# Leaving out the filler products on TensorE between the sums of the block boundaries

## The reference: what is computed

```python
def rmsnorm(x, g):
    xf = x.astype(jnp.float32)
    y = xf * lax.rsqrt(jnp.mean(xf * xf, axis=-1, keepdims=True) + EPS)
    return (y * g.astype(jnp.float32)).astype(x.dtype)

def swiglu(h, w_in, w_out):
    gate, up = jnp.split(h @ w_in, 2, axis=-1)
    return (jax.nn.silu(gate) * up) @ w_out

def sandwich(x, y_fn, g_pre, g_post, shift, scale, gate, resid_w):
    h = rmsnorm(x, g_pre) * (1.0 + scale) + shift
    return x + resid_w * gate * rmsnorm(y_fn(h), g_post)
```

## Time and profile before

| what | value |
| --- | --- |
| time, median of 3 runs | 3115.12 us (3114.57 to 3115.67) |
| span of the profiled execution | 3107.6 us |
| PE busy, share of the span | 2975.6 us, 96% |
| DVE busy | 1610.7 us, 52% |
| ACT busy | 1023.3 us, 33% |
| TensorE's mean granted clock | 0.988 of full |
| DMA, mean | 105 GB/s |

### The profile page before, as it was taken

One profiled execution on the slowest core, in us unless ns is written; L12 is line 12 of the kernel. 1 busy time (PEld: TensorE's weight loads), 2 busy tenths in 40 slices (PEclk: granted clock), 3 DMA queues, 4 the chain that ended last, 5 costly groups with the idle time before them and its releaser, 6 DMA issues.

```text
span 3107.6 us, 39441 instructions
## 1 busy us (share of the span) xinstructions
PE 2975.6 (96%) x13288; PEld 2336.5 (75%) x13288; DVE 1610.7 (52%) x2438; ACT 1023.3 (33%) x1693; POOL 167.5 (5%) x131
## 2 busy tenths in 40 slices
PE   5999999999999999999979999999999999999997
PEld 3888867677768777888858888677777778688885
DVE  5655436667444636633255553466665365465323
ACT  2322224444334323222232222344433343232321
POOL 0111010000000001110011100100000000111100
PEclk9999999999999999999989999999999999999999
DMA  5644422111212223533225543221111123154232
GB/s 200 217 175 169 142 70 82 48 48 52 65 48 88 94 77 132 185 102 102 88 84 195 189 166 112 70 68 55 48 55 62 63 78 104 48 195 164 94 96 74
DMA packets 88008, 326.76 MB, mean 105 GB/s; under 512 B 10016, under 2 KB 10400, under 8 KB 86944
## 3 DMA queue, kind: packets, MB, share of 16 engines
q1 hardware_dynamic: 87840, 324.63, 30.6%
HBM read 322.49 MB, written 2.10 MB: 104 GB/s over the span
## 4 chain that ended last, share of the span: by engine, by line
issue 65%; PE 32%; POOL 1%; DVE 1%; ACT 0%; DVEq 0%; POOLq 0%; ACTq 0%
PE bank L426 10%; PE bank L427 10%; PE bank L428 10%; POOL x L530 1%; PE bank L1580 1%; POOL rstd_tok L523 1%; PE bank L1542 0%; DVEq L1178 0%; DVE diag L1114 0%; DVE h_low L1125 0%; DVE norm_tmp L1130 0%; ACT h_high L770 0%; DVE x L1179 0%; DVE ffn_act L1281 0%; ACT ffn_high L816 0%
## 5 line engine op out<-in xcount | busy, mean ns | idle before, releaser
L426 PE MATMUL bank<-h_high,w_high 128*128 128x512 f32 x2384 | 955.7, 401 | 8.8 <-DVE h_low L1125 8.8
L428 PE MATMUL bank<-h_high,w_low 128*128 128x512 f32 x2384 | 934.9, 392 | 0.0
L427 PE MATMUL bank<-h_low,w_high 128*128 128x512 f32 x2384 | 934.3, 392 | 0.0
L410 DVE TENSOR_TENSOR w_low<-w_raw,w_high 128x1024 fp32r<-128x1024 f32 x440 | 567.9, 1291 | 698.2 <-ACT w_high L404 697.2
L404 ACT ACTIVATE w_high<-w_raw 128x1024 fp32r<-128x1024 f32 x440 | 462.3, 1051 | 402.3 <-PE bank L428 402.3
L426 PEld LDWEIGHTS bank<-h_high,w_high 128*128 128x128 f32 x2384 | 452.2, 190 | 113.6 <-DVE h_low L1125 16.2
L428 PEld LDWEIGHTS bank<-h_high,w_low 128*128 128x128 f32 x2384 | 450.9, 189 | 97.2
L427 PEld LDWEIGHTS bank<-h_low,w_high 128*128 128x128 f32 x2384 | 452.3, 190 | 91.8 <-issue 2.2
L426 PE MATMUL bank<-ffn_high,w_high 128*128 128x512 f32 x704 | 280.6, 399 | 0.0
L428 PE MATMUL bank<-ffn_high,w_low 128*128 128x512 f32 x704 | 274.2, 390 | 0.0
L427 PE MATMUL bank<-ffn_low,w_high 128*128 128x512 f32 x704 | 274.2, 389 | 0.0
(11 more groups left out here) (195 smaller groups left out, 2917.3 us busy)
## 6 DMA issues: line engine op xcount, KB each, us to landing
w_raw<-stream SPq DMA_DIRECT2D x444, 512.0 KB, 3.5
ada_raw<-ada SPq DMA_DIRECT2D x144, 512.0 KB, 3.5
ada_start<-ada SPq DMA_DIRECT2D x4, 2048.0 KB, 16.3
mixer_consts<-mixc SPq DMA_DIRECT2D x2, 1152.0 KB, 5.2
x<-x_in SPq DMA_DIRECT2D x1, 2048.0 KB, 16.3
out<-x SPq DMA_DIRECT2D x8, 256.0 KB, 2.2
lru_w<-lruw SPq DMA_DIRECT2D x2, 512.0 KB, 3.7
all_par<-pars SPq DMA_DIRECT2D x1, 163.0 KB, 2.4
```

Of the source, the lines that this page charges most:

```text
L410: eng.tensor_tensor(wL[:, slot], raw[:, slot], wH[:, slot].bitcast(F32), ALU.subtract).then_inc(lo_ready[slot].sem, 1)
L426: eng.matmul(o, a, rhs_h, start=first, stop=False)
L427: eng.matmul(o, a, rhs_l, start=False, stop=False)
L428: return eng.matmul(o, b, rhs_h, start=False, stop=last)
```

## The change

The calls of `keep_warm`, the function itself, its table of counts and the wait for the ring slot that the fillers read are taken out. Nothing else is edited: the wait on `y_saved` that stood ahead of the fillers stays.

```diff
-WARM = (10, 16, 1, 11, 6)
...
-            def keep_warm(n, times):
-
-
-                slot = (U_MIX if n == 0 else U_FFN[1]) % RING
-                for _ in range(times):
-                    pe.matmul(bank[7][:, :], wH[:, slot, 0:P], wH[:, slot, 0:T], start=True, stop=True)
-
             def end_of_boundary(l, n):
                 for j in range(4, KD):
                     sum_squares(l, sq_at(n, 0) + j, False, j == KD - 1)
                 if n < NB - 1:
                     pe.wait_ge(y_saved.sem, y_saved.at(l, 4 * n + 4))
-                    unit_ready(pe, l, U_MIX if n == 0 else U_FFN[1])
-                    keep_warm(n, WARM[0])
                 pe.wait_ge(diag_ready.sem, diag_ready.at(l, norm_at(n, 0) + 1))
                 spread(l, n, diag[:, :, :].rearrange("p t n -> p (t n)"), 5)
                 if n < NB - 1:
-                    keep_warm(n, WARM[1])
                     pre_norm(l, n)
 
             def pre_norm(l, n):
                 for j in range(KD):
                     sum_squares(l, (sq_at(n, 1) if n >= 0 else -KD) + j, j == 0, j == KD - 1)
-                    if n >= 0 and j % 2 and j < KD - 1:
-                        keep_warm(n, WARM[2])
-                if n >= 0:
-                    keep_warm(n, WARM[3])
                 pe.wait_ge(diag_ready.sem, diag_ready.at(l, (norm_at(n, 1) if n >= 0 else -1) + 1))
                 spread(l, n, diag[:, :, :].rearrange("p t n -> p (t n)"), 6)
-                if n >= 0:
-                    keep_warm(n, WARM[4])
```

## The result

The changed kernel takes 3125.75 us in the median of five runs (3123.97 to 3127.34), the kernel before 3114.66 us (3113.24 to 3115.67) beside it. The ratio is 1.0037 with a 95% interval of 1.0024 to 1.0049: slower by 7.5 to 15.3 us, with 11.1 us between the medians. The forecast was 3125.3 us.

A forecast was written before the change was run, and what follows sets the result against it. PE was taken to bound the blocks, while engines take turns at boundaries. Mixer boundaries at 2.05 us and FFN boundaries at 3.05 us, each twice, add 10.2 us: 3115.1 to 3125.3 us, range 3119.5 to 3131.5 us.

The forecast's parts named there:

- Boundary n = 2 is the model: Boundary n = 2 never had fillers; its two stretches at 0.53 clock were taken to show what the changed boundaries will do.
- sums of x: Matmul group between the two spreads of a boundary: 0.1 us lost, at most 0.6, as the clock returns within it.
- second spread: Matmul group between the last sums of x and the first product: DVE waits 0.45 us longer, between 0 and 0.95.
- first spread: Matmul group ahead of the sums of x in a boundary: DVE waits 0.3 us longer, between 0.09 and 0.94.
- entry to the mixer: First products after boundary n = 0: 1.2 us lost, between 0.65 and 1.7, with 1.0 us hidden behind DVE.
- entry to an FFN: First product to first gate after boundary n = 1, where PE is the bound: 2.2 us lost, between 1.66 and 2.72.
- 0.47 us lost for each us at half clock: Price under dense matmuls, from the FFN entry behind boundary n = 2: 1.66 us lost over some 3.5 us of products.
- The 7.5 us around the span: Time outside the profiled span, said to stay: span 3107.6 to 3117.8 us, median 3115.1 to 3125.3 us.
- The rival on the mixers' own falls: Clock falls inside the mixers land elsewhere: 5.5 us regained, 3119.8 us, chance 0.11; or worse, 3130.8 us, chance 0.11.
- A flat price for half-clock time: Rival: each us at 1.2 GHz costs 0.5 us, idle or not; four boundaries cost 40 us, 3155 us; chance 0.02.
- The clock holds: Rival: sums and spreads alone hold the full clock at n = 0 and 1, so 3115 us; chance 0.02.
- one group alone is cold: Rival: only the entries to the mixer and FFN are slow, 6.8 us in all, 3121.9 us; chance 0.07.

The follow-up runs named there:

- the second trace: The changed kernel run once more with no edit, beside the kernel before: 3126.2 us, ratio 1.0045 (1.0033 to 1.0057).

## Why the prediction was right, point by point

- *Nothing waits for the fillers.* Right: no stretch of a changed boundary got shorter by more than 0.04 us.
- *Boundary n = 2 is the model.* Right: two stretches at half clock in each changed boundary, and full clock in between from the middle of the sums of x. It hasn't "the same steps in the same times", though. In the kernel before, PE idled 5.90 us there ahead of the second spread, in the changed boundaries 2.85 us; the clock fell in both.

```profile
1585.87 2.08 PE L1542 MATMUL bank<-diag,ones 128*128 128x512 f32 x2 [5.90 <-DVE diag L1114]
```
- *The terms.* Over the eight changed boundaries of the two traces of the changed kernel:

| term | forecast | mean measured | smallest, largest |
| --- | --- | --- | --- |
| first spread | 0.3 | 0.27 | 0.0, 0.95 |
| sums of x | 0.1 | -0.03 | -0.04, -0.01 |
| second spread | 0.45 | 0.47 | 0.0, 0.95 |
| entry to the mixer | 1.2 | 1.16 | 0.47, 1.64 |
| entry to an FFN | 2.2 | 2.41 | 1.50, 2.92 |
| four boundaries | 10.2 | 10.0 | 9.6, 10.4 |

  The two bounds for an FFN entry, 1.66 and 2.72 us, were a little narrow: 1.50 and 2.92 us were seen. Entry to the mixer went from 0.47 us, below the bound of 0.65. The bound of 0.6 us for the sums was never used. The first spread's 0.3 us had a reason that doesn't hold, a short idle time ahead of it: PE idled 2.85 us ahead of either spread.
- *0.47 us lost for each us at half clock.* Right, and better than its single case could tell. In the changed kernel's two traces the clock stayed at half for 6.2, 6.2, 5.0 and 3.3 us behind the first products of the FFN entries, which lost 2.92, 2.89, 2.34 and 1.50 us: 0.45 to 0.47 us for each. The mixer entries had 5.3, 4.2, 4.8 and 2.8 us of it and lost 1.64, 1.12, 1.39 and 0.47 us. At 0.47 that leaves some 0.85 us hidden behind DVE each time, where 1.0 was forecast. What differs from entry to entry is thus how long the half clock lasts; the windows of the second trace show it for the FFN entry that lost least:

```profile
2728.41:2731.70 3.29, 3.29 (x8) 0.50 0.02 5
2731.80:2740.00 8.20, 8.20 (x37) 1.00 0.06 9
```

- *The 7.5 us around the span.* Wrong. In the changed kernel's profiled run, 3125.75 us, the span is 3123.9 us, so 1.85 us lie around it. With as much around it, the profiled execution of before was some 5 us faster than the median. One of its mixers was among the shortest seen (665.7 us in its rest); that this is all of it isn't shown. The forecast was made as a difference, so the median came out right, but the span did not: 3117.8 us was forecast and 3123.9 us profiled. That the median came within 0.5 us of 3125.3 is in part luck, since the runs give the change only as 7.5 to 15.3 us.
- *"The three runs lie within 1.1 us", so executions differ little.* Wrong. The runs of before in one later job lie between 3104.9 and 3116.6 us. Three runs were too few to see it. The rival on the mixers' own falls had the mechanism and its size right (5.5 us in a mixer): it happens in every kernel and moves single executions. Over the medians it did not add or take 5.5 us; the traces point to 1 us a mixer at most, as told above.
- *A flat price for half-clock time.* Out. By span times (1 - granted clock) times 2, the changed trace has some 156 us at half clock (clock 0.975) and that of before some 75 us (0.988). Half of the added 80 us or so would be 40 us; 11 us were measured. The half clock costs near its half where PE has dense work, by the bullet on 0.47 us, and little where PE mostly waits.
- *The clock holds; one group alone is cold.* Out: the windows show the fall in every changed boundary, and the sum with the spreads fits better than the 6.8 us of the entries alone. The experiments place 7 of 10 us or more behind the last sums of x.

## What to carry to other kernels

Work that no one needs can pay where a dense stage begins behind an idle gap: put it in the last gap ahead of the dense work, where PE idles already, and not first of all ahead of work that is bound by other engines. Six wide matmuls were enough here for most of what 46 did, because a fall of the clock in sums and spreads costs little and the clock came back in the sums. As many fillers of two columns hardly helped, and between small matmuls that follow each other the fillers cost what they gave. The length of the gap may matter too: the counts of n = 0 left 3.2 to 3.5 us idle ahead of the second spread at n = 2, and there the clock fell in two of three traces. And before a difference of 0.3% is read from single traces, one must know by how much executions of the same kernel differ.

## What the runs showed of the hardware

- A run of narrow matmuls keeps PE busy in the profile and doesn't hold its clock: 24 records in 10.1 us, busy for 8.76 us, at a granted 0.50.
- Under dense products a us at half clock cost 0.45 to 0.47 us in the four FFN entries of the changed kernel's two traces, and at the mixer's entry some 0.85 us of the loss was hidden behind DVE each time.
- The clock's falls differ between executions of the same program. The rest of a mixer, the same work each time, took 665.3 to 671.5 us over all traces. In 25 runs of the kernel before in one job the time went from 3104.9 to 3116.6 us and the mean granted clock from 0.989 to 0.985. By span times (1 - clock) times 2 that is some 25 us more at half clock for 11.7 us. Where in the program it lay isn't known for each run; two mixers with a range of 6 us each could hold most of it.
- Where and when a fall comes isn't fixed by the idle gap alone: behind the same idle 2.85 us, the first spread was slower in four of the eight changed boundaries, by 0.1 to 0.95 us, and not in the others.
